# Sixteen filler matmuls per head pair moved, one subtraction and two waits moved in the RWKV chunk loop

## The reference

```
S = S * w_t + sa (kk_t * a_t) + v_t k_t      with sa = S (-kk_t)
y_t = S r_t
y = group_norm_heads(y) * lnx_w + lnx_b;  out = (y + bonus) * g
```

## Time and profile before

| what | value |
|---|---|
| median of 3 runs | 2421.01 us (2418.49 to 2421.45) |
| the profiled execution's own time | 2421.45 us |
| its span | 2419.7 us |
| PE busy | 2358.8 us (97%) |
| DVE busy | 1379.3 us (57%) |
| POOL busy | 792.2 us (33%) |
| ACT busy | 658.5 us (27%) |
| span of PE's work on the four pairs | about 61 to 956 us |

### The profile page before, as it was taken

One profiled execution on the slowest core, in us unless ns is written; L12 is line 12 of the kernel. 1 busy time (PEld: TensorE's weight loads), 2 busy tenths in 40 slices (PEclk: granted clock), 3 DMA queues, 4 the chain that ended last, 5 costly groups with the idle time before them and its releaser, 6 DMA issues.

```text
span 2419.7 us, 33719 instructions
## 1 busy us (share of the span) xinstructions
PE 2358.8 (97%) x12944; PEld 1920.3 (79%) x12944; DVE 1379.3 (57%) x1562; ACT 658.5 (27%) x1064; POOL 792.2 (33%) x420
## 2 busy tenths in 40 slices
PE   7999999999999999999999999999999999999997
PEld 5888888888887887887787788888878787777775
DVE  7755475446536544766557745544541387657766
ACT  4311221131113112443242211111122445114541
POOL 2311231132113114113465433333334445422164
PEclk9999999999999999999999999999999999999998
DMA  3211211121111115645444111111124333211123
GB/s 140 70 53 53 71 61 45 53 70 61 53 53 64 59 49 184 204 141 203 154 131 146 55 43 49 46 43 52 43 73 135 122 122 101 64 62 37 35 79 113
DMA packets 61904, 205.22 MB, mean 85 GB/s; under 512 B 6240, under 2 KB 10464, under 8 KB 61152
## 3 DMA queue, kind: packets, MB, share of 16 engines
q1 hardware_dynamic: 40560, 138.76, 18.1%
q10 hardware_dynamic: 21232, 64.80, 7.2%
HBM read 167.36 MB, written 36.18 MB: 84 GB/s over the span
## 4 chain that ended last, share of the span: by engine, by line
PE 88%; DVE 7%; ACT 2%; DVEq 1%; issue 1%; DMA 0%; POOL 0%; ACTq 0%; POOLq 0%
PE psg L481 10%; PE psg L476 10%; PE psg L480 10%; PE psg L608 7%; PE psg L613 6%; PE psg L615 6%; PE psa L708 1%; PE psg L1208 1%; PE psg L1201 1%; PE psg L1206 1%; PE psb L695 1%; PE psg L1245 1%; PE psg L1251 1%; PE psg L1249 1%; PE psb L704 1%; PE psa L543 1%
## 5 line engine op out<-in xcount | busy, mean ns | idle before, releaser
L401 POOL CAST whi<-wraw 128x1024 fp32r<-128x1024 f32 (+1 forms) x176 | 192.2, 1092 | 1405.2 <-PE psg L608 516.3
L403 POOL TENSOR_TENSOR wlo<-wraw,whi 128x1024 fp32r<-128x1024 f32 (+1 forms) x176 | 461.7, 2623 | 25.4 <-issue 0.2
L476 PE MATMUL psg<-xhi,whi 128*128 128x512 f32 x1008 | 398.4, 395 | 3.7 <-issue 2.0
L481 PE MATMUL psg<-xhi,wlo 128*128 128x512 f32 x1008 | 400.5, 397 | 0.0
L480 PE MATMUL psg<-xlo,whi 128*128 128x512 f32 x1008 | 397.3, 394 | 0.0
L608 PE MATMUL psg<-xhi,whi 128*128 128x512 f32 x640 | 260.5, 407 | 0.0
L615 PE MATMUL psg<-xhi,wlo 128*128 128x512 f32 x640 | 259.5, 405 | 0.0
L613 PE MATMUL psg<-xlo,whi 128*128 128x512 f32 x640 | 257.3, 402 | 0.0
L476 PEld LDWEIGHTS psg<-xhi,whi 128*128 128x128 f32 x1008 | 189.2, 188 | 50.8 <-issue 5.1
L480 PEld LDWEIGHTS psg<-xlo,whi 128*128 128x128 f32 x1008 | 189.2, 188 | 48.4 <-issue 0.7
L481 PEld LDWEIGHTS psg<-xhi,wlo 128*128 128x128 f32 x1008 | 189.2, 188 | 44.7
(11 more groups left out here) (612 smaller groups left out, 4820.9 us busy)
## 6 DMA issues: line engine op xcount, KB each, us to landing
wraw<-w SPq DMA_DIRECT2D x224, 512.0 KB, 3.5
later_scratch<-stage ACTq DMA_DIRECT2D x40, 512.0 KB, 2.6
xres<-xt ACTq DMA_DIRECT2D x4, 1024.0 KB, 11.8
RV<-later_scratch SPq DMA_DIRECT2D x4, 1024.0 KB, 11.2
RG<-later_scratch SPq DMA_DIRECT2D x4, 1024.0 KB, 5.7
later_scratch<-rstage ACTq DMA_DIRECT2D x8, 512.0 KB, 2.6
mgr<-later_scratch ACTq DMA_DIRECT2D x8, 512.0 KB, 3.6
mgt<-later_scratch ACTq DMA_DIRECT2D x8, 512.0 KB, 4.5
```

Of the source, the lines that this page charges most:

```text
L401: pool.tensor_copy(whi[:, u, 0:width], wraw[:, u, 0:width])
L403: pool.tensor_tensor(wlo[:, u, 0:width], wraw[:, u, 0:width], whi[:, u, 0:width].bitcast(F32), ALU.subtract).then_inc(w_ready, 1)
L476: mm = pe.matmul(ps[:, cols], whi[:, slot, w_cols], rhs_hi(k, cols), start=(k == 0), stop=False)
L481: mm = pe.matmul(ps[:, cols], wlo[:, slot, w_cols], rhs_hi(k, cols), start=False, stop=(k == kts - 1))
```

## The change

Per pair, the filler matmuls are dealt out anew: 46 become 33 ahead of the wait for rw_prep; in each of the four groups 5 become 6 ahead of L676, 4 become 6 ahead of L683 and 5 become 6 ahead of the levels; 16 become 13 at the end of a pair, and these now stand behind the wait for y_out instead of ahead of it. The sum stays at 480. On DVE the subtraction that makes ATL moves from after the levels to right behind M, and its semaphore at_low and PE's wait for it go; in the levels, the evacuation of a filler block's halves moves from levels 2 and 3 to levels 3 and 4.

```
@@ PE, ahead of group 0
-                fill(46)
+                fill(33)
                 pe.wait_ge(sem("rw_prep"), i + 1)
@@ PE, in a group, ahead of L676, L683 and the levels
-                    fill(5)
+                    fill(6)
                     pe.wait_ge(sem("sc_out"), 16 * i + 4 * g + 4)
...
-                    fill(4)
+                    fill(6)
                     pe.wait_ge(sem("at_unit"), 4 * i + g + 1)
...
-                    fill(5)
+                    fill(6)
                     for lv in range(1, LEVELS):
@@ PE, ahead of L724
                     pe.wait_ge(sem("g0_ready"), 4 * i + g + 1)
-                    pe.wait_ge(sem("at_low"), 4 * i + g + 1)
@@ PE, end of a pair
-                fill(16)
                 pe.wait_ge(sem("y_out"), 8 * i + 8)
+                fill(13)
                 pe.wait_ge(sem("hd_sq"), 2 * i + 2)
@@ DVE, in a group
                     tt(M[:, :, :], ...).then_inc(sem("m_init"), 1)
+                    v.wait_ge(sem("at_hi"), 4 * i + g + 1)
+                    tt(ATL[:, :, :], SC[:, :, 0:P], ATH[:, :, :].bitcast(F32), SUB)
                     for lv in range(1, LEVELS):
...
-                        if lv in (2, 3):
-                            normed_half(2 * g + 1, lv - 2)
+                        if lv in (3, 4):
+                            normed_half(2 * g + 1, lv - 3)
...
-                    v.wait_ge(sem("at_hi"), 4 * i + g + 1)
-                    tt(ATL[:, :, :], SC[:, :, 0:P], ATH[:, :, :].bitcast(F32), SUB).then_inc(sem("at_low"), 1)
```

## The result

| what | before | after |
|---|---|---|
| median of the timed runs | 2421.06 us (2418.49 to 2421.45) | 2440.36 us (2438.03 to 2442.3) |
| the profiled execution's own time | 2421.45 us | 2444.97 us |
| its span | 2419.7 us | 2443.2 us |

The changed kernel takes 1.0081 times as long [1.0068, 1.0093], 19.3 us more. The forecast was 2444 with a range of 2433.5 to 2451. The three stalls of the forecast are there, each at its place and within 0.1 us of its size; the term that was mis-sized is the clock.

The account below looks back on a forecast made before the run. PE, busy 97% of the span, was taken to bound the kernel, so its waits count: 2.62 + 1.0 + 0.45 = 4.07 us per pair, 16.3 for four, plus 6 for the clock, on 2421.45: 2444, range 2434 to 2451.

Parts of the forecast that it names:

- The three stalls of the forecast: PE waits at L656 (2.62 us), L704 in group 0 (1.0) and y_out (0.45): 4.07 us per pair.
- The wait ahead of group 0: With 13 fillers gone, PE waits at L656 for rw_prep, released by DVE's BON: 2.62 us per pair.
- The fillers in the groups: The 4 fillers added per group only take back dropped ones: 0, at best a gain of 0.3 us per pair.
- the rival that hoped for a gain: PE in the groups waits for M and ATL behind modelled ends; moved blocks free it: 5.6 us faster, 2415.8, 4%.
- ATL: In group 0, POOL's subtraction holds ATL, so XM is late and PE stands at L704: 1.0 us per pair.
- The forecast's tie in group 1: POOL's cast and ATL start together; if ATL loses, XM is 0.3 us late, costing PE below 0.1 us.
- y_out: At a pair's end PE waits for ACT's output copy before its fillers: 0.45 us per pair.
- The clock: PE's clock falls after the 2.62 us wait in two of four pairs, 3.0 us each: 6 us.
- the clock holds: Rival: PE's clock does not fall after any of the four waits, 2437.8 us; chance 20%.
- ATL not held and two falls: Rival: in group 0 POOL does not hold ATL, no stall at L704; 2440 with two clock falls; chance 14%, 2434 to 2440.

Follow-up runs that it names:

- prep_26: The changed kernel with 26 fillers instead of 33 ahead of rw_prep and 27 instead of 20 in the pair's last fill: 2449.2 us, 1.0125.
- prep_38: The changed kernel with 38 fillers instead of 33 ahead of rw_prep and 15 instead of 20 in the pair's last fill: 2437.22 us, 1.0075.
- atl_only: The kernel before with only ATL moved behind M and PE's wait for at_low gone, fillers as before: 2421.7 us, 1.0006.
- yout_only: The kernel before with only the y_out wait put ahead of the 16 fillers at a pair's end: one run, 2422.72 us beside a median of 2420.32.
- fills_only: The changed kernel with ATL and the y_out wait back in their old places: 2438.88 us, 1.0069.
- busy_l852: The kernel before with four float32 matmuls that nobody needs put into PE's 4.6 us wait at L852: 2418.76 us, 0.9988.
- dummies_in_wait: The changed kernel with four float32 matmuls, whose results nobody reads, put into PE's wait for rw_prep: 2439.73 us, 1.0082.
- dummies_3: The changed kernel with three float32 matmuls for nothing put into PE's wait for rw_prep: 2438.45 us, 1.0074.
- sums_later: The kernel before with the second half's row sums (L556) behind 18 of the block's 24 matmuls instead of 12: 2417.77 us, 0.9986.
- busy_and_later: The kernel before with the edits of both busy_l852 and sums_later: 2414.76 us, 0.9974.
- stage_early: The kernel before with DVE's last two halves of stage moved ahead of its wait for gn_aff: 2422.66 us, 1.0011.

## Why the prediction was right

**The wait ahead of group 0.** 2.62 forecast, 2.62 measured (2.56 of shown idle), four times. PE had no gap ahead of L656 before, and the 0.4 us between BON and L656 was all the slack there was.

**The fillers in the groups.** 0 forecast: groups 1 to 3 grew by their four fillers, 0.93 us, and by nothing else. PE had no hidden stall there, so the rival that hoped for a gain had nothing to gain from.

**ATL.** 1.0 forecast, 1.09 measured in group 0, by the chain as forecast. That it is POOL that holds ATL is shown by moving the block: in prep_26 ATL is never long, in prep_38 it is long in group 1, in atl_only it meets only the subtraction's end. The forecast's tie in group 1 came: the two start at 159.39 and 159.38, ATL took its 0.68 us and POOL's cast 1.58 instead of 1.04, which PE does not feel.

**y_out.** 0.45 forecast, 0.45 in the traces of the changed kernel and of yout_only. In time it is not shown, as yout_only has a single run.

**The clock.** This is the term that was mis-sized. The forecast counted two falls of 3.0 us, 6 us in all; the median of the timed runs leaves 19.3 - 16.6 = 2.7 us for it. The profiled executions had three falls of four in both of the changed kernel and four of four in fills_only, but most of them cost 1.4 to 1.65 us and only one in each of the first two 2.9. By the length of group 0 the falls cost 6.2 us in one execution and 5.9 in the other. That is near 6 by errors in opposite directions: more falls, and cheaper ones. That the profiled execution's 2444.97 us meets the forecast of 2444 is luck: it is also the longest of the 21 executions on record. By the median's time alone two rivals are as near: 2437.8, the clock holds, and 2440, ATL not held and two falls. It is the traces that decide against them, by the falls and by ATL's 2.52 us with the idle at L704.

Each execution on record has its mean granted clock. It is 0.991 for the profiled one. Of the 20 others of the changed kernel one has 0.991, four 0.992, twelve 0.993 and three 0.994, and their times follow it: 2442.4 us, 2440.9 to 2442.5, 2438.9 to 2440.8, 2437.5 to 2438.0. A difference of 0.002 is 4.9 us of lost clock, give or take half of that by rounding, and the profiled execution is 4.6 us above the median. So most timed runs lost less to the clock than the profiled one. At which places they did stays open, as they have no trace. That it is the clock behind L656 at all is shown by the two kernels with dummies (no falls in eight places, group 0 always 39.8 us), and the price of a fall in time by busy_l852.

One premise did not hold in general. The forecast took from L940 that a wait of 1.89 us is not punished. Two waits stand there, 1.69 and 1.89 us, with 1.7 us of work between them. In the kernel before no fall follows. In yout_only, which is the same code but for one wait in the pairs, the waits are the same and a fall of 1.7 us follows. PE's timeline there, and busy time by stretch (clock third from the end):

```profile
1101.31 0.50 PE L940 MATMUL psg<-xhi,whi 128*128 128x512 f32 x1 [1.89 <-DVE xlo L1595]
```

```profile
1104.00:1106.00 2.00, 2.00 (x7) 1.51 (x6) 1.80 (x2) 0.11 (x1) 0.00 (x0) 0.50 0.94 373
```

So a single spared wait said little, and the falls outside the pairs change from one execution to the next as those inside do.

How the length of PE's idle time stands to what followed, in the traces of all kernels. The first four rows are the waits ahead of L656, the others the long waits behind the pairs, up to the last 20 us of the span:

| idle | where | places with a fall behind |
|---|---|---|
| 0 (matmuls in it) | L656: dummies_in_wait, dummies_3 | 0 of 8 |
| 1.4 us | L656: prep_38 | 0 of 4 |
| 2.6 us | L656: the changed kernel twice, fills_only | 10 of 12 |
| 4.2 us | L656: prep_26 | 4 of 4 |
| 1.4 us | L556: sums_later, busy_and_later | 0 of 2 |
| 1.5 us | L902: all but stage_early | 0 of 13 |
| 1.7 and 1.9 us, 1.7 us apart | L940: all | 5 of 14 |
| 2.3 us | L1245: all | 6 of 14 |
| 2.8 us | L556: all others | 11 of 12 |
| 4.6 us | L852: all but stage_early and the two with matmuls in it | 11 of 11 |

## What to carry to other kernels

Where PE is full, a distribution of filler work by hand is a set of deadlines: before moving fillers, read for each wait how long ahead of PE's arrival its releaser ends. Here that was some 0.4 us, and what was taken away beyond it, 2.62 of 3.04 us, was paid in full, then again through the clock in most pairs. Moving a block of fillers also moves what its first matmul triggers on another engine (POOL's split) and the time by which its bank must be free; check a moved operation against these new places, not the old ones. A wait that can't be removed can be filled with work of no use, which paid in the 4.6 us wait at L852 (2.8 us), or be shortened, as at L556 (3.4 us for 1.4 us less of wait, where the share of the clock is not resolved in time). In the pairs neither showed in the kernel's time: dummies must not outlast the wait, and the moved fillers brought a new stall. Whether a fall follows a wait is partly chance, so one trace with or without it is not enough to judge a wait by.

## What the runs showed of the hardware

A DVE operation with both inputs in SBUF that starts under a POOL operation ended 0.54 to 0.56 us after POOL's end (ATL 1.41, 1.65, 2.52 us instead of 0.68), while M and XM, with an input in PSUM, kept 0.68 to 0.69. It goes the other way too: POOL's cast grew from 1.04 to 1.30 us where ATL had started before it (the kernel before, 210.27) and to 1.58 where both started together (the changed kernel, 159.38), and in the earlier trace rows a subtraction of 2.39 to 2.40 us is one of 2.65.

Idle times of the same length, 2.56 us, were followed by a fall of the granted clock in ten places of twelve, and those of 2.34 us at L1245 in six executions of fourteen. A fall came in two sizes, about 1.7 and, with what was lost while PE still waited, 3.4 us of lost clock. In group 0 it cost 1.4 to 1.65 or 2.9 us of time.

A float32 matmul of 128 x 512 took 0.88 us, against 0.233 for one of the high and low parts: as a filler in a wait it is four times as coarse.
